# A two-block layer in one kernel: first norm tile by tile, RMS statistics on four columns, one scaling between the blocks

## What is computed

```python
def rmsnorm(x, g):
    xf = x.astype(jnp.float32)
    y = xf * lax.rsqrt(jnp.mean(xf * xf, axis=-1, keepdims=True) + NORM_EPS)
    return (y * g.astype(jnp.float32)).astype(x.dtype)

def first_block(x, ...):
    xn = rmsnorm(x, norm_g)
    p = xn @ w_in
    ...
    x = x + jnp.concatenate([y_rwkv, y_attn], axis=-1) @ w_out
    return rmsnorm(x, final_g)

def second_block(x, mem, ...):
    x = x + _mixer(x, mem, norm_mix_g, ...)
    x = x + _conv_ffn(x, norm_ffn_g, ...)
    return _rmsnorm(x, norm_final_g)
```

## Time and profile before

| | |
|---|---|
| median of 3 runs | 1561.13 us (1560.22 to 1562.53) |
| the profiled execution | 1561.24 us, span 1559.5 us |
| busy PE, DVE, ACT, POOL | 94%, 65%, 33%, 31% of the span |
| PE matmul records | 7442 |
| chain that ended last | PE 86%, DVE 10%, ACT 2%, rest 2% |
| granted TensorE clock, mean | 0.97 of 2.4 GHz |
| DMA | 81 GB/s on average |

### The profile page before, as it was taken

The page is one execution under the profiler, slowest core; times in us unless marked ns, Lnnn a source line. Parts: engine busy times, 40 slices in busy tenths (PEclk is TensorE's granted clock), DMA queues, the critical chain, the costliest instruction groups (busy, mean ns, idle before and its releaser), DMA issues.

```text
span 1559.5 us, 18413 instructions
## 1 busy us (share of the span) xinstructions
PE 1464.4 (94%) x7442; PEld 1159.6 (74%) x7442; DVE 1008.1 (65%) x1373; ACT 511.5 (33%) x682; POOL 486.6 (31%) x131
## 2 busy tenths in 40 slices
PE   5999888789989899999999999989988999999996
PEld 5778555377777787788888887768867888888885
DVE  3569976843773945666795995483347888884223
ACT  5433366343423333212222221422223333332211
POOL 0004021001343432334343444324342434343430
PEclk9999979799999999999999999999999999999999
DMA  6322000020232421132323333122322332332221
GB/s 179 108 81 82 0 1 1 1 83 28 80 114 77 135 81 54 55 101 88 109 81 108 89 101 102 61 81 82 107 81 70 93 108 82 108 90 93 95 74 54
DMA packets 165781, 125.58 MB, mean 81 GB/s; under 512 B 9179, under 2 KB 163586, under 8 KB 165698
## 3 DMA queue, kind: packets, MB, share of 16 engines
q1 hardware_dynamic: 163490, 122.19, 25.6%
q10 hardware_dynamic: 2208, 2.23, 0.4%
HBM read 122.31 MB, written 2.10 MB: 80 GB/s over the span
## 4 chain that ended last, share of the span: by engine, by line
PE 86%; DVE 10%; ACT 2%; issue 1%; DMA 1%; SPq 0%; DVEq 0%; ACTq 0%
PE bank L403 23%; PE bank L405 23%; PE bank L404 23%; PE bank L363 2%; PE bank L914 1%; PE bank L553 1%; PE bank L930 1%; DVE tmp L1637 1%; PE bank L512 1%; DVE x_res L2065 1%; DVE m_blk L1877 1%; PE bank L786 1%; DVE tmp L1875 1%; DVE rs_gn L2011 1%; DVE rs L1620 1%
## 5 line engine op out<-in xcount | busy, mean ns | idle before, releaser
L1113 POOL TENSOR_TENSOR w_lo<-w_raw,w_hi 128x2048 fp32r<-128x2048 f32 (+1 forms) x102 | 467.7, 4585 | 824.6 <-ACT w_hi L1160 802.5
L403 PE MATMUL bank<-op_hi,w_hi 128*128 128x512 f32 x1384 | 549.2, 397 | 23.9 <-DVE op_lo L1643 12.1
L405 PE MATMUL bank<-op_hi,w_lo 128*128 128x512 f32 x1384 | 543.2, 393 | 0.0
L404 PE MATMUL bank<-op_lo,w_hi 128*128 128x512 f32 x1384 | 543.1, 392 | 0.0
L403 PEld LDWEIGHTS bank<-op_hi,w_hi 128*128 128x128 f32 x1384 | 262.1, 189 | 86.0 <-issue 19.4
L1160 ACT ACTIVATE w_hi<-w_raw 128x2048 fp32r<-128x2048 f32 (+1 forms) x111 | 210.4, 1895 | 297.1 <-PE bank L405 297.1
L404 PEld LDWEIGHTS bank<-op_lo,w_hi 128*128 128x128 f32 x1384 | 262.2, 189 | 56.6 <-issue 1.7
L405 PEld LDWEIGHTS bank<-op_hi,w_lo 128*128 128x128 f32 x1384 | 261.8, 189 | 56.4
L2100 DVE SCALAR_TENSOR_TENSOR bank<-pad_b,par,bank 128x512 f32<-128x512 f32 x232 | 175.3, 756 | 7.8
L2264 DVE TENSOR_TENSOR tmp<-tmp,conv_f 128x512 f32<-128x512 f32 x22 | 101.6, 4617 | 16.4 <-ACT tmp L1574 16.4
L2036 DVE TENSOR_TENSOR x_res<-bank,x_res 128x512 f32<-128x512 f32 x16 | 11.0, 689 | 109.4 <-PE bank L405 109.3
(11 more groups left out here) (373 smaller groups left out, 1778.3 us busy)
## 6 DMA issues: line engine op xcount, KB each, us to landing
w_raw<-in_w_in SPq DMA_DIRECT2D x31, 1024.0 KB, 5.1
w_raw<-in_w_up SPq DMA_DIRECT2D x44, 512.0 KB, 5.0
w_raw<-in_w_in SPq DMA_DIRECT2D x33, 512.0 KB, 5.0
w_raw<-in_w_kv SPq DMA_DIRECT2D x8, 1024.0 KB, 5.2
w_raw<-in_w_down SPq DMA_DIRECT2D x8, 1024.0 KB, 5.1
w_raw<-in_w_out SPq DMA_DIRECT2D x4, 1024.0 KB, 5.0
w_raw<-in_w_att_out SPq DMA_DIRECT2D x4, 1024.0 KB, 5.1
w_raw<-in_w_a_out SPq DMA_DIRECT2D x4, 1024.0 KB, 5.1
```

Of the source, the lines that this page charges most:

```text
L403: nc.tensor.matmul(b[:, 0:width], h, xh[:, x0 + k, 0:width], start=start and k == ks[0], stop=False)
L404: nc.tensor.matmul(b[:, 0:width], h, xl(x0 + k, width), start=False, stop=False)
L405: mm = nc.tensor.matmul(b[:, 0:width], l, xh[:, x0 + k, 0:width], start=False, stop=stop and k == ks[-1])
L1113: nc.gpsimd.tensor_tensor(w_lo[u % 2][:, 0:nk, :], w_raw[u % 2][:, 0:nk, :], w_hi[u % 2][:, 0:nk, :].bitcast(F32), ALU.subtract).then_inc( ...
```

## The change

*Start.* Sum, mean, root and scaling go tile by tile; VectorE does all the scaling, in halves of 512 columns; the root's table is loaded ahead of the data by a dummy root. TensorE transposes tile by tile into eight banks. The first weight comes in two transfers of four chunks, each split on its own.

*Statistics* (`token_sums`, `spread`). VectorE adds the squares of chunks 0 to 5 into one; TensorE multiplies blocks of squares by one column of ones, so that a statistic is 128 partitions x 4 columns (token in tile, tile). Mean, reciprocal and root work on 4 columns (8 for two norms), and `spread` turns a 4-column factor into 128x512 in a bank by four matmuls with the identity. The scalings read their factor from that bank.

*Between the blocks* the operand is made from the residual in one scaling with the product of both factors and both gains. The residual's own scaling by the first norm (`normed_residual`) is done later, two chunks in each of the four steps of the second block's gated branch 2, after a second spread (`rs_y`).

```diff
-            def sum_some(key, sq, first, last):
...
+            def token_sums(key, sq):
+
+                b = bank(key)
+                for n, c in enumerate((0, CH - 2, CH - 1)):
+                    if n:
                         pe.wait_ge(sem("sq_" + key), c + 1)
+                    else:
+                        pe.wait_ge(sem("summed_" + key), 1)
+                    for t in range(NT):
+                        mm = nc.tensor.matmul(b[:, t:t + 1], sq[:, c, t * P:t * P + P], ones[:, 0:1], start=n == 0 and t == 0,
+                                              stop=n == 2, skip_group_check=True)
+                done(mm, key)
+
+            def spread(key, col, b=None):
...
+                for t in range(NT):
+                    mm = nc.tensor.matmul(b[:, t * P:t * P + P], col[:, t:t + 1].to_broadcast([P, P]), ident[:, :], start=True, stop=True)
+                done(mm, key)
...
-            for t in range(2):
-                pe.wait_ge(sem(f"x_scaled{t}"), NT // 2)
-            for c in range(CH):
-                transposes(("xnT", c), [x_scaled[:, t, c * P:c * P + P] for t in range(NT)])
+            bs = [bank(("xnT", c)) for c in range(CH)]
+            for t in range(NT):
+                for c in range(CH):
+                    if c % 4 == 0:
+                        pe.wait_ge(sem("x_scaled"), 2 * t + 1 + c // 4)
+                    mm = nc.tensor.transpose(bs[c][:, t * P:t * P + P], x_scaled[:, t, c * P:c * P + P], ident[:, :])
...
-                if i:
-                    sum_some("y", sq2, 2 * i - 2, 2 * i)
-                    sum_some("yg", sq_g, 2 * i - 2, 2 * i)
-            sum_some("y", sq2, CH - 2, CH)
-            sum_some("yg", sq_g, CH - 2, CH)
+            token_sums("y", sq2)
+            token_sums("yg", sq_g)
             for i in range(4):
                 unit_tiles("kT", i, memn_hi, plain(memn_lo), MEM)
-            ring.remove(CONV_BANK)
+                if i == 0:
+                    pe.wait_ge(sem("tok_both_ready"), 1)
...
+                    spread("rs_mix", tok_mix, ps[CONV_BANK])
             unit_tiles("u", 0, oh, ol, ready="mixn_ready")
+            spread("rs_y", tok_rs)
...
-                if i:
-                    sum_some("f", sq_f, 2 * i - 2, 2 * i)
-            sum_some("f", sq_f, CH - 2, CH)
+            token_sums("f", sq_f)
+            pe.wait_ge(sem("tok_f_ready"), 1)
+            spread("rs_f", tok_rs)
...
+                    if u == 0:
+                        sp.dma_start(w_raw[0][:, 0:CH // 2, at_:at_ + n], src[:, 0:CH // 2, :]).then_inc(sem("first_arrived"), 16)
+                        sp.dma_start(w_raw[0][:, CH // 2:CH, at_:at_ + n], src[:, CH // 2:CH, :]).then_inc(w_arrived[0], 16)
...
-            variance("y", T, 1.0 / D, NORM_EPS)
-            evac(V.tensor_tensor(rs_mix, take(dve, "yg")[:, :], rs[:, :], ALU.mult), "yg")
+            link(token_variance("y", 1.0 / D, NORM_EPS))
+            b = take(dve, "yg")
+            evac(V.tensor_tensor(tok_mix, b[:, 0:NT], tok_rs, ALU.mult), "yg")
...
             def mix_norm(c):
 
-                x = x_res[:, c, :]
-                link(V.scalar_tensor_tensor(x, x, pcol("final_g", c), rs[:, :], ALU.mult, ALU.mult))
-                if c == 0:
-                    dve.wait_ge(sem("rs_ready"), roots[0])
-                scaled_chunk("norm_mix_g_2", c, rs_mix, "mixn")
+                ins = V.scalar_tensor_tensor(tmp[c % 2][:, 0:T], x_res[:, c, :], both_g[:, c:c + 1], r_mix[:, :], ALU.mult, ALU.mult)
+                ins.then_inc(sem("mixn_scaled"), 1)
                 if c:
                     lo_chunk(c - 1, "mixn")
...
                         conv_taps(8)
+                        normed_residual(2 * i, 2 * i + 2)
```

More of the change, by code:

```diff
@@ L382, in next_unit @@
                 return u
-            def sum_some(key, sq, first, last):
[L387 to L392, removed]
-                        pe.wait_ge(sem("sq_" + key), c + 1)
-                        mm = nc.tensor.matmul(b[:, :], ones[:, :], sq[:, c, :], start=False, stop=c == CH - 1)
-                    done(mm, key)
+            def token_sums(key, sq):
+                b = bank(key)
+                for n, c in enumerate((0, CH - 2, CH - 1)):
+                    if n:
+                        pe.wait_ge(sem("sq_" + key), c + 1)
+                    else:
[5 more added lines that the diff above has]
+            def spread(key, col, b=None):
+                if b is None:
+                    b = bank(key)
+                for t in range(NT):
+                    mm = nc.tensor.matmul(b[:, t * P:t * P + P], col[:, t:t + 1].to_broadcast([P, P]), ident[:, :], start=True, stop=True)
+                done(mm, key)
             def tile(b, u, col, width, xh, xl, x0=0, start=True, stop=True, ks=None):
@@ L437, in _ @@
             done(nc.tensor.transpose(b[:, 0:CH], gain_rows[0:CH, :], ident[0:CH, 0:CH]), "gain")
-            for t in range(2):
-                pe.wait_ge(sem(f"x_scaled{t}"), NT // 2)
-            for c in range(CH):
-                transposes(("xnT", c), [x_scaled[:, t, c * P:c * P + P] for t in range(NT)])
-            oh, ol = op_hi, plain(op_lo)
-            unit_tiles("qd", 0, oh, ol, ready=lambda k: evacuated(pe, ("xnT", k)))
+            bs = [bank(("xnT", c)) for c in range(CH)]
[4 more added lines that the diff above has]
+                    mm = nc.tensor.transpose(bs[c][:, t * P:t * P + P], x_scaled[:, t, c * P:c * P + P], ident[:, :])
+                    if t == NT - 1:
+                        done(mm, ("xnT", c))
+            oh, ol = op_hi, plain(op_lo)
+            u = unit[0]
+            unit[0] += 1
+            bs = [bank(("qd", 0, m)) for m in range(2)]
+            for k in range(CH):
+                evacuated(pe, ("xnT", k))
+                if k == 0:
+                    pe.wait_ge(sem("first_lo"), 1)
+                elif k == CH // 2:
+                    pe.wait_ge(lo_ready, u + 1)
+                for m in range(2):
+                    mm = tile(bs[m], u, m * P, T, oh, ol, start=k == 0, stop=k == CH - 1, ks=[k])
+                    if k == CH - 1:
+                        done(mm, ("qd", 0, m))
+            unit_last[u] = ("qd", 0, 1)
             unit_tiles("kvi", 0, oh, ol)
@@ L1162, in _, with root @@
             roots = [0]
[L1164 to L1168, removed]
+            def root(t=rs[:, :], done="rs_ready"):
+                if done == "rs_ready":
+                    roots[0] += 1
+                    act.wait_ge(sem("var_ready"), roots[0])
+                else:
+                    act.wait_ge(sem(done.replace("ready", "var")), 1)
+                A(t, t, ACT.Sqrt).then_inc(sem(done), 1)
+            act.wait_ge(sem("consts"), 1)
+            A(misc[:, 127:128], ones[:, 0:1], ACT.Sqrt)
             for t in range(NT):
@@ L1174, in _ @@
                 act.wait_ge(sem("sq_x"), t + 1)
[L1175 to L1179, removed]
+                act.wait_ge(sem("x_var"), t + 1)
+                A(rs_x[:, t:t + 1], rs_x[:, t:t + 1], ACT.Sqrt).then_inc(sem("x_rs"), 1)
+            act.wait_ge(sem("first_arrived"), 16)
+            A(w_hi[0][:, 0:CH // 2, :], w_raw[0][:, 0:CH // 2, :], ACT.Copy).then_inc(sem("first_hi"), 1)
             evacuated(act, "gain")
@@ L1504, in _ @@
             u_gate(0)
+            evac(A(rs[:, :], take(act, "rs_y")[:, :], ACT.Copy), "rs_y")
             mem_query(0)
@@ L2249, in _ @@
             lo_chunk(CH - 1, "ffn")
+            release("rs_f")
             for i in range(FC):
```

115 lines of the change are left out of this document (83 added, 32 removed).

## The result

| | kernel before | changed kernel |
|---|---|---|
| median of 20 runs each | 1563.05 us | 1554.2 us |
| ratio of the runs, 95% interval | | 0.9944, 0.9928 to 0.996 |
| profiled execution, its span | 1561.24, 1559.5 | 1560.24, 1558.5 |
| mean granted clock | 0.973 | 0.961 |

The change gives 8.7 us where 16.2 were forecast: the direction is right and the size is not; 1554.2 lies above the range. (8.7 is by the ratio, 8.85 by the medians.) The profiled execution of the changed kernel is itself 6 us slower than its median, so its parts have to be read one by one.

What follows compares the result with a forecast made beforehand. TensorE, busy nearly all the time, was taken as the bound; gains of 2.8 (start), 5.0 (between the blocks), 4.3 (before the feed-forward) and 4.1 (end) sum to 16.2, so 1561.24 becomes 1545.0 us, range 1539 to 1551.

Steps and rivals of the forecast that it cites:

- Start: Up to the first product: TensorE starts near 17.5 instead of 21.84; gain 2.8 us, ends 1.3 and 4.3.
- The 1.5 taken off for a cold TensorE: At the start: TensorE at half clock for 3.1 us does 1.55 us of work, so gain 2.8 instead of 4.3.
- Between the blocks: From the last `wout` unit through `u` 0: fewer sums, less waiting for operands; gain 5.0 us, ends 3.7 and 6.0.
- a group of four products is eight records, so I take 1.02: Price in us of each narrow sums group, from the two-column product at full clock; upper end 1.72, lower 0.7.
- the prediction's own sign of being wrong: For the narrow sums: the prediction is wrong if narrow records pace at over 0.2.
- the 2.3 us that the half clock in `u` 0 was to have cost before: In `u` 0 of the kernel before: the wait brought the clock to 0.52 for 6.7 us, costing some 2.3.
- Before the feed-forward: Sums inside go (1.7), shorter path from last square to first scaling (2.6); gain 4.3 us, ends 2.8 and 5.6.
- half clock after the wait as before: Before the feed-forward: half clock behind TensorE's wait taken as unchanged within the 4.3 us gain; 5.6 with no clock loss.
- End: End of the kernel: sums inside go (1.7), shorter path from square to first scaling (2.4); gain 4.1 us, 3.4 to 4.8.
- The moved scalings: Gated branch: eight residual scalings absorbed by VectorE's idle time and seven banks, cost nothing; up to 40 us without that cover.
- Small products are dear: Rival, all three sums places: every narrow group costs 1.72 and more; gain some 8 us, 1553; chance 8%.
- the row at 204.49: Profile row of the kernel before, cited for the rival that every narrow group costs 1.72 and more.

Runs made afterwards that it cites:

- e1: The kernel before with the new start alone (norm tile by tile, first weight in halves): 1559.15 us, ratio 0.997.
- e3: The changed kernel with its small sums multiplied into all 128 columns of ones instead of one: 1545.97 us, ratio 0.9903 to the kernel before.
- e2: The changed kernel with the start of before, so the sums in four columns alone: 1555.79 us, ratio 0.9953 to the kernel before.
- e4: The changed kernel with `kT` 0 ahead of the small sums and the spread behind `kT` 1: 1549.21 us, ratio 0.9905 to the kernel before.
- e11: The changed kernel with weight splits of `kT` 2, `kT` 3, `u` 0 and the unit behind made by VectorE instead of GpSimd: 1548.06 us, ratio 0.9902.
- e5: The kernel before with VectorE adding squares of six chunks, three products per statistic instead of five, still 512 wide: 1556.62 us, ratio 0.9957.
- e6: The changed kernel with its small sums multiplied into 32 columns of ones instead of one: 1551.34 us, ratio 0.9917 to the kernel before.

## Why the prediction was wrong

- **Start**, forecast 2.8 with 4.3 if TensorE were warm: 3.75 in the changed kernel's trace, 5.0 to 6.35 in the nine experiments' that have the new start; about 0.5 of each belongs to the trace of before. The first product came at 16.55 instead of 17.5. The 1.5 taken off for a cold TensorE was too much: the changed kernel's trace ran its first products at half clock (0.77 at 16.55) for 3.4 us, e1 too, and the other eight not at all.
- **Between the blocks**, forecast 5.0, measured 0.2. The step that failed is the price "a group of four products is eight records, so I take 1.02" for five groups in a row. It holds for the first (0.95) and for none after 504.4: the 24 records of `sq_g` took 4.92, 1.9 more, and `kT` 0 took 8.4, 2.6 more. At 0.205 a record this is the prediction's own sign of being wrong. I had priced the clock only after the wait in `u` 0, and looked for its cause in waits alone. The rest of this part stood up: with all columns e3 has 4.96, `kT` 0 at 502.9 when its lead at 473 is taken out (500.00 + 2.89), 503 expected, and a wait of 2.71 for chunk 3, some 3 expected. Three `op_lo` were held, chunks 0, 1 and 3, as worked out. One price in it no run shows: the 2.3 us that the half clock in `u` 0 was to have cost before. e1 has the same wait there (4.65) and 3.4 us of half clock instead of 6.8, and its unit ends no sooner: its lead is 3.95 on both sides of the unit.
- **Before the feed-forward**, forecast 4.3, measured 1.5; 2.4 to 2.5 in e2, e4 and e11. Two steps failed. The narrow groups and the spread ran at half clock: the second group took 3.58, the spread 2.08, and the last square's end and the first scaling lie 6.0 us apart where 3.8 was forecast (3.6 in e3). And "half clock after the wait as before" can't be taken over even with all columns: e3 has the same 6.8 us of it, but its shorter wait (2.32 for 7.20) puts 5.91 us of products into them, where before had 3.02. By my estimate that costs (5.91 - 3.02) / 2 = 1.4 us: the first product comes 4.5 us earlier in e3, counted from the lead that it had at 1130, and 3.16 are left behind the stretch. e5 has 1.36 for the sums inside (1.7 expected).
- **End**, forecast 4.1, measured 3.1; 4.21 in e3.
- **The moved scalings**, forecast 0: 0.01 to 0.04 between 590 and 1130, in every trace; TensorE's waits for VectorE between 553 and 1125 are 6.1 us for 6.0.
- **The chances.** "Small products are dear" had 8% and 1553, and 1554.2 came. It named the row at 204.49 and took it for a price of its own; that row was a group at half clock, behind a wait of 3.41, and it doesn't tell which of the two, group or wait, goes with the half clock. "Against: the same form at 175.20 took 1.02" was one group in otherwise dense work. A row of more than eight such records stood nowhere in what I had read of before, and my bounds held both prices of a group, but not that a row of them changes the price of the unit behind it.

With the one edit of e3 the sum comes near the measured time, 15.2 us by the ratio and 17.3 by the medians against 16.2, but by luck in part: its trace has 5.2, 5.0, 3.2 and 4.2 for 2.8, 5.0, 4.3 and 4.1, a start sized too small against a feed-forward part sized too large. What stays open: why 16 one-column records as filler do no harm where 48 in a row do (no run varies their number); why the half clock before the feed-forward and at the end differs between traces of the same code; and whether the second column of the table is chance. Its 12 traces lie 3.9 us above the one of before on average; the median of before in 20 runs lies 1.8 us above its profiled execution, so a part of it is that this execution was a good one.

## What to carry to other kernels

When a change makes products on TensorE smaller, read the granted clock of the stretch and of the unit behind it, not the duration of one product: the small form was 0.1 us cheaper per eight records and cost 4.8 us between the blocks, 6 to 8 us in the whole kernel. Where the result has room, multiply into all 128 columns and read those that are needed. Where two-input work of VectorE in SBUF stands on the path while GpSimd works, give GpSimd's part to VectorE for that stretch: it took half as long and held nobody.

## What the runs showed of the hardware

- TensorE's granted clock fell to 1.2 GHz while it was busy without a gap (100% of 497.6 to 516.4 in e4), within a row of 48 records whose products give one column. Between the blocks, in the changed kernel's order, with its wait of 1.7 to 1.8 us, it fell with one column and with 32 (e6), and with 128 it stayed at 2.4 GHz (e3).
- Records of 128x1 and of 128x128 take nearly the same time: 0.95 and 1.05 us for eight.
- The granted clock differs between executions of one kernel: the changed kernel's 20 run from 1549.99 us at a mean of 0.968 to 1569.4 us at 0.954. Among the 13 traces, 4 have a stretch of 13.7 us at half clock in the scan (from 387 to 391 us on), in code that is the same in all, worth about 7 us; the profiled execution of the changed kernel is one of them.
- A wait of TensorE can hide the half clock behind it: before the feed-forward, 6.8 us at half clock held 3.02 us of products in the kernel before and 5.91 in e3.
